# A hybrid decoder layer: SyncE's block copies two units earlier, norm logarithms ahead of exponentials, a paired small projection, and memory keys turned by VectorE

## The reference

```python
h = h + 0.5 * rmsnorm(swiglu(rmsnorm(h, n_ffn1_pre), w_ffn1_gu, w_ffn1_down), n_ffn1_post)
u = rmsnorm(h, n_mix_pre)
(gla_q, gla_k, gla_v, gla_lr, gla_r, gdn_qkv, gdn_b, gdn_a, gdn_z,
 xa_q, gate_logits) = jnp.split(u @ w_in, idx, axis=-1)
# three mixers on column groups of u @ w_in:
#   gated linear attention (4 heads, 64-token chunks), output rmsnorm * silu(gla_r)
#   gated delta rule (8 heads; solves a unit lower triangular system per chunk)
#   softmax cross-attention to 256 memory tokens, keys and values from
mk, mv = jnp.split(rmsnorm(mem, mem_norm) @ w_mem_kv, 2, axis=-1)
mixed = (g_a * y_gla + g_b * y_gdn + g_c * y_xa) @ w_out      # g: sigmoid(gate_logits)
h = h + rmsnorm(mixed, n_mix_post)
h = h + 0.5 * rmsnorm(swiglu(rmsnorm(h, n_ffn2_pre), w_ffn2_gu, w_ffn2_down), n_ffn2_post)
```

## Time and profile before

| | |
|---|---|
| median of 3 runs | 2496.83 us (2495.46 to 2498.13) |
| the profiled execution | 2495.89 us, of which its span is 2494.2 us |
| TensorE | busy 2467.6 us (99%), granted clock 0.999 |
| VectorE, ScalarE, GpSimd | busy 1397.4, 1235.8 and 430.8 us |
| DMA | 498.53 MB, mean 200 GB/s |

### The profile page before, as it was taken

One profiled execution on the slowest core, in us unless ns is written; L12 is line 12 of the kernel. 1 busy time (PEld: TensorE's weight loads), 2 busy tenths in 40 slices (PEclk: granted clock), 3 DMA queues, 4 the chain that ended last, 5 costly groups with the idle time before them and its releaser, 6 DMA issues.

```text
span 2494.2 us, 32008 instructions
## 1 busy us (share of the span) xinstructions
PE 2467.6 (99%) x11197; PEld 2044.4 (82%) x11197; DVE 1397.4 (56%) x1698; ACT 1235.8 (50%) x1502; POOL 430.8 (17%) x853
## 2 busy tenths in 40 slices
PE   9999999999999999999999999999999999999998
PEld 7888888888888888888888888888888888888887
DVE  5555555555556456676676564465655555555444
ACT  6444444444445456757585444444644444444443
POOL 6212121122101003223231120010121211211000
PEclk9999999999999999999999999999999999999999
DMA  7777677677768656555564766765676776767654
GB/s 251 211 201 210 202 208 203 202 214 210 215 211 266 195 171 171 167 161 163 158 178 135 215 207 196 225 221 187 215 211 200 204 206 201 210 201 252 194 190 157
DMA packets 305838, 498.53 MB, mean 200 GB/s; under 512 B 28236, under 2 KB 102096, under 8 KB 304976
## 3 DMA queue, kind: packets, MB, share of 16 engines
q1 hardware_dynamic: 282336, 457.85, 61.7%
q0 software_dynamic: 23120, 38.95, 4.9%
q10 hardware_dynamic: 288, 0.52, 0.1%
HBM read 471.39 MB, written 8.52 MB: 192 GB/s over the span
## 4 chain that ended last, share of the span: by engine, by line
PE 91%; POOL 2%; DVE 2%; DMA 2%; ACT 2%; issue 1%; SPq 0%; DVEq 0%; POOLq 0%; ACTq 0%
PE acc L676 86%; POOL mkh L636 1%; POOL mkh L639 1%; PE acc L718 1%; PE acc L701 1%; DMA post_a<-n_ffn_post 1%; DMA sq<-mk_scratch 1%; DVE wlo L1580 1%; ACT whi L1105 0%; DMA raw<-w_ffn_gu 0%; PE mix L736 0%; PE mix L945 0%; DMA raw<-w_in 0%; PE mix L839 0%; PE mix L979 0%
## 5 line engine op out<-in xcount | busy, mean ns | idle before, releaser
L1580 DVE TENSOR_TENSOR wlo<-raw,whi 128x1024 fp32r<-128x1024 f32 x860 | 1052.1, 1228 | 898.6 <-ACT whi L1105 895.3
L1105 ACT ACTIVATE whi<-raw 128x1024 fp32r<-128x1024 f32 x860 | 909.8, 1060 | 1177.2 <-PE acc L676 1134.7
L676 PE MATMUL acc<-whi,x_hi 128*128 128x512 f32 x1616 | 629.6, 390 | 0.0
L676 PE MATMUL acc<-whi,x_lo 128*128 128x512 f32 x1616 | 628.7, 389 | 0.0
L676 PE MATMUL acc<-wlo,x_hi 128*128 128x512 f32 x1616 | 628.7, 389 | 0.0
L676 PE MATMUL acc<-whi,u_hi 128*128 128x512 f32 x896 | 357.4, 399 | 1.9 <-ACT pr L1187 1.3
L676 PEld LDWEIGHTS acc<-whi,x_lo 128*128 128x128 f32 x1616 | 303.3, 188 | 63.2
L676 PEld LDWEIGHTS acc<-wlo,x_hi 128*128 128x128 f32 x1616 | 303.3, 188 | 62.7
L676 PEld LDWEIGHTS acc<-whi,x_hi 128*128 128x128 f32 x1616 | 303.3, 188 | 62.5
L300 POOL DMA_DIRECT2D nat<-nat x416 | 204.0, 498 | 848.4 <-DVE nat L1702 676.2
L676 PE MATMUL acc<-whi,u_lo 128*128 128x512 f32 x896 | 349.4, 390 | 0.0
(11 more groups left out here) (360 smaller groups left out, 1627.8 us busy)
## 6 DMA issues: line engine op xcount, KB each, us to landing
raw<-w_ffn_gu SPq DMA_DIRECT2D x352, 512.0 KB
raw<-w_ffn_down SPq DMA_DIRECT2D x176, 512.0 KB
raw<-w_in SPq DMA_DIRECT2D x224, 256.0 KB
raw<-w_in SPq DMA_DIRECT2D x96, 512.0 KB
raw<-w_mem_kv SPq DMA_DIRECT2D x32, 512.0 KB
raw<-w_out SPq DMA_DIRECT2D x32, 512.0 KB
nat<-nat POOLq DMA_DIRECT2D x416, 32.0 KB, 3.7
raw<-w_in SPq DMA_DIRECT2D x64, 128.0 KB
```

The lines of the kernel that those rows point to most:

```text
L676: ins = nc.tensor.matmul(acc[:, par, t, :], x[:, k0 + k, cols], w[:, s, k, :], start=first and k == 0 and m == 0, stop=last and k == UK - ...
L1105: act(whi[:, s], raw[:, s], ACT.Copy).then_inc(hi_ready, 1)
L1580: tt(wlo[:, s], raw[:, s], whi[:, s].bitcast(fp32), ALU.subtract).then_inc(lo_ready, 1)
```

## The change

Four edits. SyncE's `blocks_out` and `blocks_in` stand behind the loads of units 16 and 18 in place of 18 and 19. ScalarE's step 24 does both logarithms, then both exponentials. The small projection has `wsmh` and `wsml` side by side in one tensor of 64 columns, `wsm2`: `u_hi` and `u_lo` are each multiplied with both (2 x 16 products with 64 output rows), and in place of the transposes two products with `fold`, two identities one above the other, turn the result and add the two halves (so `u_lo * wsml` is now in the sum). The memory keys are turned by VectorE in 32x32 blocks from `mkn` into `mkT`, and GpSimd's DMAs put the blocks in their places: eight to each half, each of 32 partitions by 16 blocks by 32 numbers.

```diff
-OUT_UNIT, IN_UNIT = 18, 19
+OUT_UNIT, IN_UNIT = 16, 18
...
-             ("mkT", [P, 4, SEQ], fp32), ("wsm", [P, KT_D, 32], fp32), ("wsmh", [P, KT_D, 32], f32r),
-             ("wsml", [P, KT_D, 32], f32r), ("small_T", [32, SEQ], fp32)],
+             ("mkT", [P, 4, SEQ], fp32), ("wsm", [P, KT_D, 32], fp32), ("wsm2", [P, KT_D, 64], f32r),
+             ("small_T", [64, SEQ], fp32)],
...
+        wsmh, wsml = wsm2[:, :, 0:32], wsm2[:, :, 32:64]
...
@@ gpsimd
                 pl.wait_ge(sem("mk_ready"), i + 1)
-                pl.dma_start(mk_v[:, 4 * i:4 * i + 4, :], mkT[:, :, :]).then_inc(sem("mk_stored"), 16)
+                src = mkT[:, :, :].rearrange("p k (j t l) -> p (k j) t l", t=NT, l=32)
+                for q in range(4):
+                    for t in range(NT):
+                        dst = mk_dram[i * CW:(i + 1) * CW, t * P + q * 32:t * P + (q + 1) * 32].rearrange("(b r) m -> r b m", r=32)
+                        pl.dma_start(dst, src[32 * q:32 * q + 32, :, t, :]).then_inc(sem("mk_stored"), 16)
@@ tensor, memory
-                    if j in (12, 25):
-
-                        pe.wait_ge(acc_out[0], q + j // 16 + 1)
-                        pe.wait_ge(t_lo, half_tiles(T_U + 4))
-                        if j == 25:
-                            pe.wait_ge(sem("mk_ready"), 1)
-                        v = mix[:, 2:4, :].rearrange("p b (k s) -> p (b k) s", s=SEQ)
-                        for blk in range(4):
-                            for t in range(NT):
-                                ins = nc.tensor.transpose(v[:, blk, t * P:(t + 1) * P], mkn[:, t, blk * P:(blk + 1) * P], ident)
-                        ins.then_inc(sem("mk_done"), 1)
@@ tensor, small_steps
-                        for m, (x, w) in enumerate(((u_hi, wsmh), (u_hi, wsml), (u_lo, wsmh))):
-                            ins = nc.tensor.matmul(mix[0:32, 0, 0:SEQ], w[:, k, :], x[:, k, :],
-                                                   start=k == 0 and m == 0, stop=k == KT_D - 1 and m == 2)
+                        for m, x in enumerate((u_hi, u_lo)):
+                            ins = nc.tensor.matmul(mix[0:64, 0, 0:SEQ], wsm2[:, k, :], x[:, k, :],
+                                                   start=k == 0 and m == 0, stop=k == KT_D - 1 and m == 1)
...
-                        ins = nc.tensor.transpose(mix[:, 1, t * 32:(t + 1) * 32], small_T[:, t * P:(t + 1) * P], ident[0:32, 0:32])
+                        ins = nc.tensor.matmul(mix[:, 1, t * 32:(t + 1) * 32], small_T[:, t * P:(t + 1) * P], fold[:, :],
+                                               start=True, stop=True)
@@ scalar, memory
-                    if j in (12, 25):
-                        ac.wait_ge(sem("mk_done"), 1 + j // 16)
-                        if j == 25:
-                            ac.wait_ge(sem("mk_stored"), 16)
-                        act(mkT[:, :, :], mix[:, 2:4, :].rearrange("p b (k s) -> p (b k) s", s=SEQ), ACT.Copy).then_inc(sem("mk_ready"), 1)
@@ scalar, mixer_steps
                     act(gss[:, :], gss[:, :], ACT.Ln, scale=1.0 / GLA_DV, bias=cst[:, 0:1]).then_inc(sem("gln"), 1)
+                    need("oss_ready")
+                    act(oss[:, :], oss[:, :], ACT.Ln, scale=1.0 / GDN_D, bias=cst[:, 0:1]).then_inc(sem("oln"), 1)
                     need("gln")
                     act(gss[:, :], gss[:, :], ACT.Exp, scale=-0.5).then_inc(sem("grn_ready"), 1)
-                    need("oss_ready")
-                    act(oss[:, :], oss[:, :], ACT.Ln, scale=1.0 / GDN_D, bias=cst[:, 0:1]).then_inc(sem("oln"), 1)
@@ vector, memory
+                    if j in (12, 25):
+
+                        ve.wait_ge(acc_out[0], QB["mem"] // 2 + j // 16 + 1)
+                        if j == 25:
+                            ve.wait_ge(sem("mk_stored"), 8 * 16)
+                        v = mkT[:, :, :].rearrange("p k (j t l) -> p t k j l", t=NT, l=32)
+                        for t in range(NT):
+                            ins = nc.vector.transpose(v[:, t], mkn[:, t, :].rearrange("p (k j l) -> p k j l", j=4, l=32))
+                        ins.then_inc(sem("mk_ready"), 1)
                     if j == SPLIT_SMALL:
                         ve.wait_ge(*once("wsm_hi"))
-                        tt(wsml[:, :, :], wsm[:, :, :], wsmh[:, :, :].bitcast(fp32), ALU.subtract).then_inc(once("wsm_lo")[0], 1)
+                        tt(fold[:, :], ident[0:64, 0:32], ident[0:64, 32:64], ALU.add)
+                        tt(wsml, wsm[:, :, :], wsmh.bitcast(fp32), ALU.subtract).then_inc(once("wsm_lo")[0], 1)
```

More of the change, by code:

```diff
@@ L151, in hybrid_layer @@
         o_hi, o_lo, msum, mtmp = ov["o_hi"], ov["o_lo"], ov["msum"], ov["mtmp"]
-        mkn, mvn, mkT, wsm, wsmh, wsml = (ov[k] for k in ("mkn", "mvn", "mkT", "wsm", "wsmh", "wsml"))
+        mkn, mvn, mkT, wsm, wsm2 = (ov[k] for k in ("mkn", "mvn", "mkT", "wsm", "wsm2"))
+        wsmh, wsml = wsm2[:, :, 0:32], wsm2[:, :, 32:64]
         small_T, vec, convn, post_a = ov["small_T"], ov["vec"], ov["convn"], ov["post_a"]
@@ L241, in hybrid_layer @@
         cst = sb("cst", [P, 2])
+        fold = sb("fold", [64, 32])
         eye = sb("eye", [P, BLOCK])
@@ L582, in _ @@
                 pl.wait_ge(sem("mk_ready"), i + 1)
-                pl.dma_start(mk_v[:, 4 * i:4 * i + 4, :], mkT[:, :, :]).then_inc(sem("mk_stored"), 16)
+                src = mkT[:, :, :].rearrange("p k (j t l) -> p (k j) t l", t=NT, l=32)
[3 more added lines that the diff above has]
+                        pl.dma_start(dst, src[32 * q:32 * q + 32, :, t, :]).then_inc(sem("mk_stored"), 16)
                 pl.wait_ge(acc_out[1], QB["mem"] // 2 + i + 1)
                 pl.dma_start(mv_v[:, :, i * CW:(i + 1) * CW], mvn[:, :, :]).then_inc(sem("mv_stored"), 16)
-            pl.wait_ge(sem("mk_stored"), 2 * 16)
+            pl.wait_ge(sem("mk_stored"), 16 * 16)
             pl.wait_ge(sem("mv_stored"), 2 * 16)
@@ L1273, in tasks @@
                         ac.wait_ge(sem("small_in"), 6 * 16)
-                        act(wsmh[:, :, :], wsm[:, :, :], ACT.Copy).then_inc(once("wsm_hi")[0], 1)
+                        act(wsmh, wsm[:, :, :], ACT.Copy).then_inc(once("wsm_hi")[0], 1)
                     if j % U_D == U_D - 1:
@@ L1279, in tasks @@
                         if c == 2:
-                            ac.wait_ge(sem("mk_done"), 1)
+                            ac.wait_ge(sem("mk_ready"), 1)
                         if c == 3:
@@ L1301, in small_steps @@
                     ac.wait_ge(*once("small_done"))
-                    act(small_T[:, :], mix[0:32, 0, 0:SEQ], ACT.Copy).then_inc(once("small_T_ready")[0], 1)
+                    act(small_T[:, :], mix[0:64, 0, 0:SEQ], ACT.Copy).then_inc(once("small_T_ready")[0], 1)
                 if j == 2:
```

## The result

The changed kernel takes **2483.32 us** (median of 5 runs, 2483.05 to 2486.30) beside 2496.49 us of the kernel before on the same chip (5 runs, 2495.34 to 2498.13): a ratio of 0.9949, with a 95% interval of 0.9938 to 0.9960, or 13.2 us less. The forecast was 2480.6, in a range of 2477.5 to 2489.5, so the side and the range held, and the time is 2.7 us above the forecast. Two of the further runs of the kernel before were far slower (2744.33 and 6472.16 us) and are in no comparison.

The account below looks back on a forecast made before the run. TensorE was taken as the bound. Gains of 9.7 + 2.4 + 1.6 + 1.8 + 0.9 - 0.2 = 16.2 us took the profiled 2495.89 to 2479.7, plus 0.94 for the median: 2480.6 us, range 2477.5 to 2489.5.

Parts of the forecast that it names:

- What bounds the kernel: TensorE, busy 2467.6 of 2494.2 us: only work taken off it or idle time taken from it can move the end.
- The block DMAs, 4 x 2.42 = 9.7 us: SyncE's earlier block copies let GpSimd start 4.2 us earlier, so TensorE's four waits on sq at L945 vanish: 9.7 us.
- Rival (a): Eight fetches in the air together land later; 1.2 us of wait stays at each L945 place: 2485.4 us, chance 0.20.
- The collisions: GpSimd's small steps running into VectorE's splits: about five in place of three, taken at 0.9 us each.
- The logarithms, 2.4 us: ScalarE's step 24 needs two table loads, not four, so four L676 waits on pr and gates vanish: 4 x 0.61 us.
- restarts, 0.9: Eight TensorE waits and two L825 runs vanish, each with a slow start of 0.09 us: 0.9 us gained.
- The memory keys, 1.6 us: VectorE's transposes replace TensorE's L825 products at two places: 2 x 0.79 us; missing cover would return 1.4 us a place.
- The small projection, 1.8 us: On TensorE, 32 products replace 48: 16 x 0.1135 us saved; turning by fold gives 0.2 us back.
- The store of the keys, at 33 ns a run: GpSimd's stores in 128-byte runs, priced from wsm loads, ask for 17 us of the DMA engines and stay hidden.
- Rival (c): Short store runs starve the weight loads; slower from 88 ns a run, 2523 us at 130 ns; chance 0.07.
- (b): Moving the block DMAs brings nothing because GpSimd's own fetches, slowed by SyncE's, land late: 2490.3 us, chance 0.05.
- (d): ScalarE's new order still has four table loads, so none are saved: 2483 us, chance 0.01.

Follow-up runs that it names:

- 17 and 18: Changed kernel with SyncE's block stores behind unit 17's load and the fetches behind unit 18's: 2481.33 us, ratio 0.9938.
- the best kernel: Changed kernel with SyncE's block stores behind unit 16's load and fetches behind unit 17's, not 18's: 2478.19 us, ratio 0.9926.

## Why the prediction was right, and where it was not

**What bounds the kernel** held: TensorE is 99% busy before and after, and all of the 12.8 us can be found between the starts of its products.

**The block DMAs, 4 x 2.42 = 9.7 us** is the term that was mis-sized: 4.9 us came. Rival (a), a remnant, which had a chance of 0.20, is what happened, and the range held because it was made wide enough for it. 1.2 us was left at a place on average, just the size that (a) was given, but by luck: GpSimd started 1.9 us later than forecast in the first group, and a cheaper chain gave 1.1 of it back. The step that failed is "data is in at 963.5 + 1.9" with "GpSimd's own fetches are then last and it starts at 966.0". It carried over how long the fetches took in the trace of before, where they had one unit's load in front of them. Moving the stores ahead made the loads of units 17 and 18 wait together and go out together, right ahead of the fetches, and these took 4.5 and 4.9 us from issue to landing, where the working had 3.5 for GpSimd's and 1.9 behind the last issue for SyncE's. The issues themselves came when the working said. The runs with 16 and 17, and 17 and 18, bear this out: with one load between stores and fetches the median landings are 2.6 to 3.5 us, and with 16 and 17 the whole 9.7 us comes. The reason that (a) gave for itself, eight fetches in the air together, is not enough: the best kernel has them together as well, and 0.7 us on SyncE's landings (3.3 against 2.6) is the most that it shows.

**The collisions** were counted a little too dear: in the first group four and not five, 0.85 to 1.07 us each against 0.9, and a chain of 14.4 us for 15.5. Without these 1.1 us the wait there would be 1.9 and not 0.84. The Trainium skill's "SBUF — State Buffer", section "Who interferes with whom", has the later of the two instructions blocked fully; L642, which began with the split, ended 0.17 us behind it, as the earlier trace rows show for L639, so the trace agrees with the page; no step lost the 1.33 us that the prediction took as the fullest case.

**The logarithms, 2.4 us, and restarts, 0.9**: the waits on pr and gates are gone, and with restarts the trace has 3.0 us. Half a microsecond more came at L880, which the forecast had not seen. Taken out of the best kernel it costs 3.0 (profiled executions) to 4.3 us (medians).

**The memory keys, 1.6 us**: 1.6 in the trace, 1.2 alone and 2.6 out of the best kernel. VectorE and ScalarE had the room; the 1.4 us that a missing cover would have cost do not show.

**The small projection, 1.8 us**: 1.8 in the trace, 2.1 alone and 2.0 out of the best kernel; a weight load of 64 columns costs nothing, since the products still start 0.1135 us apart. The fold gives back 0.3 and not 0.2.

**The store of the keys, at 33 ns a run**, was the uncertain price, and it is 5 to 6 ns. Between before and after the share grows by 0.03 over 35 us and 0.08 over 20, 2.7 us of all engines. Rival (c) needed 88 ns. The rows of the wsm loads were a poor neighbour: if a load's run costs 6 ns as a store's does, which is not shown, 2048 runs ask for 0.8 us of sixteen engines, and nearly all of their 7.0 us was something else; what, no run here shows. The Trainium skill's "DMA: Bandwidth & Descriptors", section "Specifications", has runs under 512 bytes read, modified and written; if these were, no cost of it shows in the times of the best kernel and of the one that stores twice.

**Rivals (b) and (d)** are out: GpSimd started 12.1 us after lmat where 14.4 was before and 10.2 forecast, and the table loads are two.

**The time**: 2480.6 was forecast and 4.8 us of wait stayed; 2485.4 was the price of that, and the 0.5 at L880 and the 0.7 and 0.5 at two untouched steps bring it to 2483.7, beside the 2483.3 measured. The 1.2 us of the untouched steps are luck: they differ from one profiled execution to the next. Taking the data's arrival from a row with another queue in front of it was a choice, and the margin it had was nil (982.6 against 982.62), so the remnant should have been the forecast.

## What to carry to other kernels

The time from issue to landing of a small DMA is no property of the DMA: the same fetches of 64 KB took 2.6 to 4.9 us here (medians). It depends on what stands ahead of it, and moving a wait within a queue in order changes that, because all that had to wait goes out in one burst behind it. Before such an edit, look at what lies between the wait and the transfer that something is waiting for, and keep it to the least. Here one unit's load less, by one number, was worth 5.1 us. And where a busy TensorE has waits of some microseconds, small edits are measured after these waits are gone, not before: the same order of logarithms was worth 0.5 us with them and 3 to 4 without.

## What the runs showed of the hardware that was not expected

**A short wait of TensorE costs more than its length.** With a wait of 3.8 to 4.0 us the granted clock was 0.50, the lower of its two levels, for over 6 us from where TensorE started again, in all four places, and the products started 0.43 us apart in place of 0.23: some 2.9 us more a place, without the slow restart. Behind waits of 2.2 to 2.6 us it happened in four places of sixteen (three of four in one profile, one of four in another, none in that of before and that of the small projection alone), at 1.6 us each. Behind waits of 1.6 us and less it was never seen in these profiles. The products ahead of the wait are the same ones in all of these kernels. The Trainium skill's "TensorE: Matmul & The Clock Gate", section "The HAM clock gate (the "warmup" mystery)", has the array at 1.2 GHz after idle time; these rows agree with that level.

The clock on record for every run fits it: the 40 runs of the kernels whose profile has no wait on sq above 1.6 us all have 0.999, the 49 of before 0.998 or 0.999 with 1.4 us between the medians of the two groups, and those with the 4 us waits 0.994. It is not the only source of spread: the seven runs of the block DMAs alone lie 4.5 us apart, all at 0.999.

**Stores of 128-byte runs are cheap here**, 6 ns a run and engine, the 128 bytes included, and sixteen of 64 KB land in 4.6 us each (median) while the weights pass.
